# Router weights in four column groups of TensorE, token rows moving, and one product that adds the four parts

## The reference, cut to what matters

```python
h = rms_norm(x, norm_mix[l])
x = x + mixer(h, ...)                    # ends with  o @ w_out
h = rms_norm(x, norm_ffn[l])
aff = jax.nn.softmax((h @ w_router).astype(jnp.float32), axis=-1)   # 1024 tokens x 16 experts
gate, idx = lax.top_k(aff.T, cap)        # 64 tokens for each expert
g, u = xe @ w_gate, xe @ w_up            # xe = the chosen rows
y = (silu(g) * u) @ w_down * gate        # added back at idx
```

## Time and profile before

| what | before |
|---|---|
| median of 3 runs | 2786.36 us (2785.28 to 2787.68) |
| profiled execution, its time | 2786.92 us |
| its span (first to last instruction) | 2785.1 us |
| TensorE busy | 2600.1 us, 93% |
| VectorE busy | 938.6 us, 34% |
| ScalarE busy | 442.0 us, 16% |
| GpSimd busy | 566.7 us, 20% |

### The profile page before, as it was taken

One profiled execution on the slowest core, in us unless ns is written; L12 is line 12 of the kernel. 1 busy time (PEld: TensorE's weight loads), 2 busy tenths in 40 slices (PEclk: granted clock), 3 DMA queues, 4 the chain that ended last, 5 costly groups with the idle time before them and its releaser, 6 DMA issues. The chain is left out here.

```text
span 2785.1 us, 25308 instructions
## 1 busy us (share of the span) xinstructions
PE 2600.1 (93%) x8968; PEld 1294.7 (46%) x8968; DVE 938.6 (34%) x1610; ACT 442.0 (16%) x1119; POOL 566.7 (20%) x714
## 2 busy tenths in 40 slices
PE   8999999978999999999799989999969999999994
PEld 4456555544444444444345444544534444444442
DVE  2464355343232232332134223422243233232332
ACT  2164154110000000000113221322100000000001
POOL 2275266210000000000025322531000000000002
PEclk9999999988999999999899999999979999999997
DMA  6000031346989889887400112023268988989975
GB/s 188 22 1 20 0 136 42 116 186 244 320 312 324 315 312 327 311 317 267 160 22 14 61 48 82 18 75 140 93 237 315 320 308 322 318 316 316 321 257 180
DMA packets 176951, 535.08 MB, mean 192 GB/s; under 512 B 32865, under 2 KB 46689, under 8 KB 176865
## 3 DMA queue, kind: packets, MB, share of 16 engines
q1 hardware_dynamic: 167360, 499.35, 49.2%
q0 software_dynamic: 9504, 34.61, 5.2%
HBM read 490.92 MB, written 44.56 MB: 192 GB/s over the span
## 5 line engine op out<-in xcount | busy, mean ns | idle before, releaser
L1661 PE MATMUL bank<-ring,arena 128*128 128x512 f32 x3072 | 1334.1, 594 | 3.7 <-issue 1.9
L1661 PEld LDWEIGHTS bank<-ring,arena 128*128 128x128 f32 x3072 | 580.2, 191 | 710.7 <-issue 708.5
L866 PE MATMUL bank<-ring,arena 128*128 128x512 f32 (+1 forms) x1024 | 429.7, 577 | 3.0 <-DMA ring<-in_w_in_cd 2.2
L1495 POOL TENSOR_SCALAR arena<-arena 128x512 f32<-128x512 f32 (+2 forms) x256 | 325.0, 1287 | 197.6 <-DVE arena L1378 197.0
L883 PE MATMUL bank<-arena,ring 128*128 128x512 f32 x752 | 333.0, 598 | 7.9 <-DVE arena L1334 7.9
L866 PEld LDWEIGHTS bank<-ring,arena 128*128 128x128 f32 x1024 | 194.5, 193 | 215.0 <-issue 207.9
L1791 POOL DMA_INDIRECT residual<-arena x32 | 51.0, 1595 | 1028.4 <-DVE arena L1742 1028.4
L883 PEld LDWEIGHTS bank<-arena,ring 128*128 128x128 f32 x752 | 141.2, 191 | 181.1 <-issue 169.7
L1736 DVE RECIPROCAL arena<-arena 128x512 f32<-128x512 f32 x64 | 214.6, 3353 | 2.2
L1724 DVE COPY arena<-bank 128x512 f32<-128x512 f32 x66 | 45.6, 692 | 415.7 <-PE bank L1650 415.7
L1222 ACT ACTIVATE arena<-arena 128x256 f32<-128x256 f32 (+2 forms) x192 | 113.1, 590 | 309.3 <-DVE arena L1368 309.3
(11 more groups left out here) (152 smaller groups left out, 1556.1 us busy)
## 6 DMA issues: line engine op xcount, KB each, us to landing
ring<-in_w_gate SPq DMA_DIRECT2D x64, 2048.0 KB, 7.9
ring<-in_w_up SPq DMA_DIRECT2D x64, 2048.0 KB, 9.2
ring<-in_w_down SPq DMA_DIRECT2D x64, 2048.0 KB, 9.5
ring<-in_w_in_cd SPq DMA_DIRECT2D x6, 2048.0 KB, 17.6
ring<-in_x_in SPq DMA_DIRECT2D x16, 512.0 KB, 4.4
residual<-ring SPq DMA_DIRECT2D x16, 512.0 KB, 2.8
normed<-ring SPq DMA_DIRECT2D x16, 512.0 KB, 2.6
arena<-residual SPq DMA_DIRECT2D x16, 512.0 KB, 6.6
```

The costliest lines, as they stand in the source:

```text
L866: mm = eng.matmul(bank[banks_of(piece)[k]][0:rows, 0:wide], lhs(c), rhs(c), start=(c == 0), stop=(c == chunks - 1))
L1495: pool_s.done(eng.tensor_scalar(p_of(i, e), p_of(i, e), stat[:, PLACE[i] % 4, 4 + e:5 + e], None, ALU.mult), f"scale{e}", *piece)
L1661: mm = eng.matmul(bank[first_bank + b][:, :], lhs[:, 4 * half + c, :], piece[k][:, c, b * BANK:(b + 1) * BANK], start=(half == 0 and c == ...
```

## The change

The stationary and the moving side of the router product change places. The router weights are laid out in 32 columns per chunk (16 of weights, 16 of zeros), so `o_router` becomes 128 x 256 and is zeroed by GpSimd (in piece `yn` of tile 0) before the load fills its 16 columns of each chunk. Chunk c is loaded into column group c mod 4 (32 columns of the array), the 128 token columns of `hoT` move, and the result, four partial sums of 32 rows x 128 tokens, stands in bank 6. ScalarE copies it to `partial`. A new piece `rsum` multiplies `partial` (stationary, 128 x 128) by `rows_to_slots`, which now has an identity in each of the four groups, and so adds the four parts and turns them to 128 tokens x 16 in bank 5. The softmax follows this product. `rsum` of tile n-3 stands between `ya` and `yb` of tile n. The router load moves behind the store of tile 0's normed rows in SP's queue; the wait for the constants (`const_in`) becomes one for the gain alone, and the router has a semaphore of its own. The transposes into bank 5 wait until the softmax has read the sum of two tiles before. The start stage copies two more identities.

```diff
+                eng.tensor_copy(rows_to_slots[64:80, :], ident[64:80, 64:80])
+                eng.tensor_copy(rows_to_slots[96:112, :], ident[96:112, 96:112])
...
                     if n < N:
                         yield "ya", n
+                    if 3 <= n:
+                        yield "rsum", n - 3
+                    if n < N:
                         yield "yb", n
...
-                "rlog": {"pe": ("logits",), "act": ("exp",), "dve": ("max", "recip", "aff"), "pool": ()},
+                "rlog": {"pe": ("quarters",), "act": ("take",), "dve": (), "pool": ()},
+                "rsum": {"pe": ("logits",), "act": ("exp",), "dve": ("max", "recip", "aff"), "pool": ()},
...
+                    if n == 0:
+                        eng.wait_ge(router_zero, 1)
+                        eng.dma_start(o_router[:, :, 0:E], at(w_router, layer * D * E, [[E, P], [P * E, DC], [1, E]])).then_inc(router_in, 16)
...
-                eng.wait_ge(pe_s.sem, pe_s.after("logits", "rlog", N - 1))
+                eng.wait_ge(pe_s.sem, pe_s.after("quarters", "rlog", N - 1))
...
                             wait_taken(eng, ("rturn", i - 1) if i else ("turn", 1, STEP[-1]), k)
+                            if k and i >= 2:
+                                wait_taken(eng, ("rsum", i - 2))
...
-                        product(piece, 0, E, lambda c: hoT[i % 2][:, c, :], lambda c: o_router[:, c, :], DC, "logits")
+                        for c in range(DC):
+                            g = 32 * (c % 4)
+                            mm = eng.matmul(bank[6][g:g + 32, 0:P], o_router[:, c, :], hoT[i % 2][:, c, :], start=(c < 4), stop=(c >= 4))
+                        pe_s.done(mm, "quarters", *piece)
+                    elif what == "rsum":
+                        eng.wait_ge(act_s.sem, act_s.after("take", "rlog", i))
+                        wait_taken(eng, ("rturn", min(i + 1, N - 1)), 1)
+                        if i == N - 1:
+                            wait_taken(eng, ("rsum", i - 1))
+                        pe_s.done(eng.matmul(bank[5][:, 0:E], partial[i % 2], rows_to_slots[:, :], start=True, stop=True), "logits", *piece)
...
                     elif what == "rlog":
+                        eng.wait_ge(pe_s.sem, pe_s.after("quarters", *piece))
+                        if i >= 2:
+                            eng.wait_ge(pe_s.sem, pe_s.after("logits", "rsum", i - 2))
+                        act_s.done(eng.activation(partial[i % 2], bank[6][:, 0:P], ACT.Copy), "take", *piece)
...
                         if i == 0:
                             eng.memset(aff_rows[:, 0:96], 0.0).then_inc(aff_zero, 1)
+                            eng.wait_ge(aff_zero, 1)
...
+                            eng.memset(o_router, 0.0).then_inc(router_zero, 1)
+                            eng.wait_ge(router_zero, 1)
```

More of the change, by code:

```diff
@@ L559, in wait_taken @@
                     taken = {"qd": [(act_s, "take")], "kd": [(dve_s, "take")],
-                             "rlog": [(act_s, "exp")], "raff": [(dve_s, "aff")]}[what]
+                             "rlog": [(act_s, "take")], "rsum": [(act_s, "exp")], "raff": [(dve_s, "aff")]}[what]
                 for steps, mark in taken:
@@ L613, in mixer @@
                 assert pT_at + 2048 <= ARENA
-                o_gain, o_router = vm.rearrange("p a b -> p (a b)")[:, 0:D], vm.rearrange("p a b -> p (a b)")[:, D:D + DC * E]
+                o_gain, o_router = vm.rearrange("p a b -> p (a b)")[:, 0:D], vm.rearrange("p a b -> p (a b)")[:, D:D + DC * 32]
+                partial = [vw.rearrange("p a b -> p (a b)")[:, k * P:(k + 1) * P] for k in range(2)]
                 at_qm, at_km, at_qw = 2 * DC * SEQ, 2 * DC * SEQ + H * SEQ, 2 * DC * SEQ + 2 * H * SEQ + T * H * HD
@@ L666, in mixer @@
             if not ab:
-                o_gain, o_router = gain, hT[:, 0, 0:DC * E]
+                o_gain, o_router = gain, hT[:, 0, 0:DC * 32]
+                partial = [hT[:, 1, k * P:(k + 1) * P] for k in range(2)]
             o_router = o_router.rearrange("p (c n) -> p c n", c=DC)
@@ L1244, in act @@
                         if i >= 2:
-                            eng.wait_ge(pe_s.sem, pe_s.after("logits", "rlog", i - 2))
+                            eng.wait_ge(pe_s.sem, pe_s.after("quarters", "rlog", i - 2))
                         act_s.done(eng.activation(hoT[i % 2][:, 0:4, :], bank[4][:, :].rearrange("p (c n) -> p c n", c=4), ACT.Copy),
@@ L1412, in dve @@
                         dve_s.done(eng.tensor_copy(hoT[i % 2][:, 4:8, :], bank[5][:, :].rearrange("p (c n) -> p c n", c=4)), "take", *piece)
-                    elif what == "rlog":
+                    elif what == "rsum":
                         eng.wait_ge(pe_s.sem, pe_s.after("logits", *piece))
                         if i >= 2:
-                            eng.wait_ge(act_s.sem, act_s.after("exp", "rlog", i - 2))
+                            eng.wait_ge(act_s.sem, act_s.after("exp", "rsum", i - 2))
                             eng.wait_ge(pe_s.sem, pe_s.after("turn", "raff", i - 2))
-                        dve_s.done(eng.tensor_reduce(st[:, i % 2, 9:10], bank[6][:, 0:E], AX.X, ALU.max, negate=True), "max", *piece)
+                        dve_s.done(eng.tensor_reduce(st[:, i % 2, 9:10], bank[5][:, 0:E], AX.X, ALU.max, negate=True), "max", *piece)
                         eng.wait_ge(act_s.sem, act_s.after("exp", *piece))
@@ L1539, in pe @@
                 eng.wait_ge(dve_s.sem, dve_s.after("spread"))
-                eng.matmul(bank[0][:, 0:E], spread_i, rows_to_slots[:, :], start=True, stop=True)
-                pe_s.done("slots", eng.matmul(bank[1][:, 0:E], spread_v, rows_to_slots[:, :], start=True, stop=True))
+                eng.matmul(bank[0][:, 0:E], spread_i, rows_to_slots[0:48, :], start=True, stop=True)
+                pe_s.done("slots", eng.matmul(bank[1][:, 0:E], spread_v, rows_to_slots[0:48, :], start=True, stop=True))
             def dve(eng):
```

21 lines of the change are left out of this document (13 added, 8 removed).

## The result

The changed kernel takes **2774.06 us** (median of 4, 2772.46 to 2774.43) against 2786.35 us before (median of 4): a ratio of 0.9955, 95% interval 0.9943 to 0.9967. It is 12.3 us faster. The forecast was 2783.5 us within 2776 to 2791, so the time lies outside the range, a little beyond the rival R1 (2775.8). The profiled execution took 2774.43 us, its span is 2772.6 us.

A forecast was written before the change was run, and what follows sets the result against it. TensorE, busy 93% of the span, was taken as the bound. Rounds saving 2.7 us, tails saving 0.5 and small edits losing 0.3 summed to -2.8 us, giving 2783.5 us, range 2776 to 2791.

The forecast's parts named there:

- R1: Rival for the router's quarter products: four column groups stream at once, 27 ns an instruction, 2775.8 us; chance 0.17.
- the spacing of the quarter instructions: Router products on TensorE: starts 54 ns apart, as with two groups, so 16 instructions take 0.86 us.
- The gaps: TensorE going into the narrow 32-column form and out: 0.31 to 0.43 us a visit, taken as 0.36.
- The adding product's price: Two instructions with 128 weight columns between two output products: 0.21 us, not below 0.1, not above 0.4.
- The tail: End of each layer's output stage: max of tile 7 at 13.25 us; 0.5 us saved over both layers.
- The two waits for bank 5: Tail: tile 5's adding product waits for VectorE's copy (5.16 us); the second four transposes until the bank is free, ending at 7.25.
- The small edits: Two more first-stage VectorE copies lose 0.34 us; GpSimd's zeroing (0.3 to 0.5 us) and the moved router load cost nothing.
- R4: Rival: the clock falls inside a round, 6.9 us per fall over one output half, say 2795 us; chance 0.04.
- R2: Rival for the quarter products: four groups do not overlap, 107 ns an instruction, 2799.0 us; chance 0.06.
- R3: Rival: switching to the narrow form or the adding product costs twice, 0.72 and 0.4 us, 2790.1 us; chance 0.13.

The follow-up runs named there:

- the free bank: Changed kernel with the adding product in bank 0 or 2 instead of bank 5, its waits for bank 5 gone: 2771.77 us.
- the reordered kernel: Changed kernel with the eight router products reordered (chunks 0, 4, 1, 5, 2, 6, 3, 7), so that same-group products are neighbours: 2773.78 us.

## Why the prediction was wrong

- **The failed step is the spacing of the quarter instructions.** The prediction put it at 54 ns because "the two instructions of one product stand next to each other and use the same group", and because starts were taken to keep the program's order. The second condition is wrong: with same-group products as neighbours four groups still ran at once, and with blocks of four products three waiting instructions were overtaken. The value products could not tell, since two groups allow no more than a pair. Measured: 16 instructions in four steps of 109 ns, 0.44 us, 27 ns each, R1's number; R1 as a whole (2775.8 us) came within 1.7 us. This is 0.42 us in ten sets (4.2 us), and twice that in four sets of the tails (3.4 us): 7.6 of the 9.4 us between forecast and measurement.
- **The gaps were mis-sized.** 0.69 - 0.44 = 0.25 us a visit, not 0.36: 0.11 in ten sets, 1.1 us. With two groups and with one it is the same, 0.24 us (1.11 - 0.87 and 1.98 - 1.74), so it does not hang on the overlap. Why it is less than in the round trip between value products and transposes is open: a narrower weight load with less of it exposed would explain it, but no run separates that.
- **The adding product's price was right**: 0.22 against 0.21, and the doubled one shows it again.
- **The tail was right in its waits and wrong in its sum.** The copy of bank 5 ended at 5.16 us as written, the adding product started at 5.31 (5.2), and its first max stood at 5.71 (5.85); from there two sets of 1.02 us stood where 1.9 had been put. So max of tile 7 came at 11.59 us in layer 0 and 11.18 in layer 1 instead of 13.25. Tile 7's first transposes came 0.91 us later than before, forecast 0.7. The two waits for bank 5 that the prediction named cost 1.19 us in layer 0, by the free bank, and 1.2 to 1.5 in layer 1 at like clock. The prediction priced the tail at the low clock from its first adding product on (0.57 us); that product took 0.37 and 0.36 us.
- **The small edits** were right: 0.37 us for the two copies (0.34), GpSimd's zeroing 0.31 us each, and the router load of layer 1, issued at 1895.1 us, landed 10.9 us later, long before the first quarter product at 1925.84.
- **The clock** stayed at 1.00 in the rounds, so R4 did not come. R2's mechanism, as the kernel with one group has it, is slower than the kernel before (2790.4 us), but the four groups do overlap. R3 was not seen: the gap was 0.25 us and the adding product 0.22.
- **The Trainium skill.** TensorEngine Tiling (Array Packing), section Theoretical Speedup, with its up to 4x at 32 columns, is confirmed for streaming: 1.74, 0.87 and 0.44 us for one, two and four groups. The forecast had given this rule a chance of 0.17. The page TensorE: Matmul & The Clock Gate, Part 3, section The mechanism, says that matmuls keep program order in start and end. By the order of starts the reordered kernel's set would have taken 1.42 us; it took 0.44, so here the measurement decides against it, for instructions on different column groups.

## What to carry to other kernels

If a product has at most 32 columns on one side, make that side the stationary one and deal the chunks over the four column groups: against one group the streaming cost falls fourfold (here 1.74 to 0.44 us; the products of before took 1.70), and what is added is about 0.25 us for going into the narrow form and out, and 0.22 us if the parts must be added by a product. A row measured with two groups is a bound for four, not a price. When a step is put into a queue at a new place, ask which bank it writes: in the full rounds bank 5 was free and cost nothing, in the tail it held back the transposes and what followed by 1.2 us, and a free bank gave that back. Compare tails only at like granted clock: the same kernel's differed by 0.6 and 0.9 us with it.

## What the runs showed of the hardware that was not expected

- Instructions for a free column group start although an earlier one waits for its own group: batches of four within 20 ns (40 ns in the second order), 109 ns apart. It reached over three waiting instructions of a group and no further (first start of group 1, at 467 ns, with the fifth of group 0, at 461), but over three of each of three groups.
- Inside a batch the starts are 7 ns apart for each product of distance in the program.
- At the end of the output stage the granted clock was 0.75 and 0.81; with 2.6 us of otherwise useless products in the tail's wait it was 1.00 in all four tails recorded, and 0.67 to 0.81 in all ten of the changed and the free-bank kernels without them. The tails were 0.6 and 0.8 us shorter with them in the first comparison; in the second 0.6 in layer 0 (10.41 to 9.82) and none in layer 1 (9.73 to 9.82), where the clock without them had been 0.81. The extra products gain little where the clock falls less, since they delay the transposes.
